# Hybrid attention layer: the multiplication of the softmax weights by 1/row sum moved to ScalarE in both attentions

## What is computed

```python
proj = h @ w_in
# forgetting attention (FoX), 8 heads of 128, causal, blocks of 128 queries
s = einsum('bqhd,bkhd->bhqk', qi, k) * scale + ci - cum_k
p = softmax(where(mask, s, NEG_INF));  o_fox = einsum('bhqk,bkhd->bqhd', p, v)
# sliding window (SWA), 16 query heads of 64, 4 key heads, window 128, a sink per head
s = einsum('bnqhgd,bnkhd->bnhgqk', qb, kk) * d**-0.5 - slope * dist
p = softmax(concat([s, sink]))[..., :-1];  o_swa = einsum('bnhgqk,bnkhd->bnqhgd', p, vv)
y = (o_fox * silu(g_fox)) @ w_br_fox ... ; out = layer_norm(ALPHA * x + gate * (merged @ w_out)) * g + b
```

## Time and profile before

| what | value |
|---|---|
| median of 3 runs | 2979.22 us (2978.62 to 2983.83) |
| profiled execution, its own time | 2981.71 us |
| its span in the trace | 2980.0 us |
| TensorE busy | 2716.4 us, 91% |
| VectorE busy | 1806.2 us, 61% |
| ScalarE busy | 1120.8 us, 38% |
| GpSimd busy | 363.3 us, 12% |
| sliding window attention | about 915 to 1520 us of the span |
| forgetting attention | about 1520 to 2190 us |

### The profile page before, as it was taken

The page is one execution under the profiler, slowest core; times in us unless marked ns, Lnnn a source line. Parts: engine busy times, 40 slices in busy tenths (PEclk is TensorE's granted clock), DMA queues, the critical chain, the costliest instruction groups (busy, mean ns, idle before and its releaser), DMA issues. The chain is left out here.

```text
span 2980.0 us, 39132 instructions
## 1 busy us (share of the span) xinstructions
PE 2716.4 (91%) x12241; PEld 2183.8 (73%) x12241; DVE 1806.2 (61%) x2769; ACT 1120.8 (38%) x2081; POOL 363.3 (12%) x357
## 2 busy tenths in 40 slices
PE   4888999899998999999969999999969999999895
PEld 2367786777876777777758888888747888888684
DVE  5655565895566777777746666566555455644335
ACT  4422234423234444444434444444433332334111
POOL 0200001100010000000001111111130001023002
PEclk9999999999999999999989999999979999999997
DMA  6455542465664333333374443443464454555442
GB/s 227 155 211 218 190 169 99 120 147 149 169 140 103 111 111 111 111 110 111 104 276 106 112 101 93 104 106 90 106 180 134 147 168 168 172 168 177 135 143 102
DMA packets 303094, 421.29 MB, mean 141 GB/s; under 512 B 16256, under 2 KB 227264, under 8 KB 298432
## 3 DMA queue, kind: packets, MB, share of 16 engines
q1 hardware_dynamic: 273504, 353.51, 36.4%
q0 software_dynamic: 16480, 58.75, 10.5%
q10 hardware_dynamic: 13056, 8.39, 1.0%
HBM read 301.05 MB, written 119.55 MB: 141 GB/s over the span
## 5 line engine op out<-in xcount | busy, mean ns | idle before, releaser
L1542 PE MATMUL pA<-b_hi,w_hi 128*128 128x512 f32 x1008 | 401.6, 398 | 64.2 <-DVE ctile L1112 37.0
L1542 PE MATMUL pC<-b_hi,w_hi 128*128 128x512 f32 x1008 | 403.4, 400 | 31.0 <-DVE ctile L1112 16.6
L1542 PE MATMUL pA<-b_hi,w_lo 128*128 128x512 f32 x1008 | 398.9, 396 | 0.0
L1542 PE MATMUL pA<-b_lo,w_hi 128*128 128x512 f32 x1008 | 397.2, 394 | 0.0
L1542 PE MATMUL pC<-b_hi,w_lo 128*128 128x512 f32 x1008 | 396.2, 393 | 0.0
L1542 PE MATMUL pC<-b_lo,w_hi 128*128 128x512 f32 x1008 | 395.4, 392 | 0.0
L1105 DVE TENSOR_TENSOR w_lo<-w_sum,w_hi 128x512 fp32r<-128x512 f32 x336 | 254.5, 762 | 175.9 <-ACT w_hi L758 173.9
L151 ACT CAST w_hi<-w_raw 128x1024 fp32r<-128x1024 f32 x128 | 134.9, 1054 | 424.7 <-PE zP L2209 208.8
L758 ACT CAST w_hi<-w_sum 128x512 fp32r<-128x512 f32 x336 | 208.9, 622 | 202.6 <-DVE w_sum L1100 106.9
L1542 PEld LDWEIGHTS pA<-b_hi,w_hi 128*128 128x128 f32 x1008 | 191.7, 190 | 120.5 <-issue 51.9
L156 DVE TENSOR_TENSOR w_lo<-w_raw,w_hi 128x1024 fp32r<-128x1024 f32 x128 | 159.5, 1246 | 195.4 <-ACT w_hi L151 194.4
(11 more groups left out here) (252 smaller groups left out, 4892.5 us busy)
## 6 DMA issues: line engine op xcount, KB each, us to landing
w_raw<-in_w_in_dram SPq DMA_DIRECT2D x84, 1024.0 KB, 7.6
proj_scratch<-ctile SPq DMA_DIRECT2D x84, 512.0 KB, 2.7
proj_scratch<-ctile POOLq DMA_DIRECT2D x84, 512.0 KB, 5.6
bg_raw<-in_w_ada_dram SPq DMA_DIRECT2D x64, 512.0 KB, 5.1
w_raw<-in_w_out_dram SPq DMA_DIRECT2D x64, 512.0 KB, 3.9
w_raw<-in_w_br_swa_dram SPq DMA_DIRECT2D x32, 512.0 KB, 3.9
w_raw<-in_w_br_fox_dram SPq DMA_DIRECT2D x32, 512.0 KB, 3.8
aux<-proj_scratch SPq DMA_DIRECT2D x64, 256.0 KB, 3.9
```

Source lines behind the costliest of these rows:

```text
L1542: last = nc.tensor.matmul(BANKS[k][:], w[:, j, :], b[:, j, :], start=(k < 4 and n == 0), stop=(n == 11), skip_group_check=True)
```

## The change

The multiplications by `row_inv` leave GpSimd (L703, L715) and VectorE (L1337). ScalarE does them as copies with a scale that is read per partition from `row_inv`: four instructions of 128x256 in each half of a unit, one of 128 x 128(i+1) in each block of a head. In a unit they stand one `after` step behind the exponentials. In a head they stand directly behind the exponential. In the second half of a unit VectorE now forms `row_inv` before its `half_out(0)`, and ScalarE's copies stand before its own `half_out(0)`. GpSimd keeps its DMAs.

```diff
--- before.py
+++ after.py
@@ -696,13 +696,6 @@
                 gate_out(1)
                 group_out(35, 2 * (35 - QKV - 6))
 
-                with pool.Fori(0, 32) as s:
-                    pool.wait_ge(s_inv, s + 1)
-                    for i in range(2):
-                        w = sp_w[:, i].rearrange("p k t -> p (k t)")
-                        last = nc.gpsimd.tensor_tensor(w, w, row_inv[:, i:i + 1].broadcast_to([P, 2 * P]), ALU.mult)
-                    last.then_inc(s_norm, 1)
-
                 for row in range(2):
                     pool.wait_ge(stored[row], 16 * GROUPS)
 
@@ -710,10 +703,6 @@
                     q = 3 * h + Q_FOX
                     dst = 6 * h + B_G
                     for i in range(8):
-                        pool.wait_ge(f_inv, 8 * h + (i + 1))
-                        w = fp_w[:, 0:i + 1].rearrange("p j t -> p (j t)")
-                        nc.gpsimd.tensor_tensor(w, w, row_inv[:, 0:1].broadcast_to([P, (i + 1) * P]),
-                                                ALU.mult).then_inc(f_norm, 1)
                         if i == 2:
                             add_group(q, 0, dst)
                         if i == 3:
@@ -907,6 +896,12 @@
                                                  accum_out=row_sum[:, i:i + 1])
                         nc.scalar.activation(sink_exp[:], sink_exp[:], ACT.Exp).then_inc(s_exp, 1)
 
+                    def normalise(e):
+                        act.wait_ge(s_inv, 2 * u + (e + 1))
+                        for i in range(4):
+                            ins = nc.scalar.activation(sp_w[:, i], sp_w[:, i], ACT.Copy, scale=row_inv[:, i:i + 1])
+                        ins.then_inc(s_norm, 1)
+
                     def turned_high(e):
                         for k in range(2):
                             act.wait_ge(s_turned, 4 * u + (2 * e + k + 1))
@@ -921,11 +916,14 @@
                     at = SWA_AFTER[par]
                     passed(at[0], at[1])
                     exponentials(0)
-                    passed(at[1], at[2])
+                    passed(at[1], at[1] + 1)
+                    normalise(0)
+                    passed(at[1] + 1, at[2])
                     turned_high(0)
                     passed(at[2], at[3])
                     exponentials(1)
                     passed(at[3], at[4])
+                    normalise(1)
                     half_out(0)
                     passed(at[4], at[5])
                     turned_high(1)
@@ -970,6 +968,11 @@
                         nc.scalar.activation(fp_w[:, 0:i + 1, :].rearrange("p j t -> p (j t)"),
                                              sP[:, :, :].rearrange("p a t -> p (a t)")[:, 0:(i + 1) * P], ACT.Exp,
                                              bias=neg_max[:, 0:1], accum_out=row_sum[:, 0:1]).then_inc(f_exp, 1)
+
+                    def normalise(i):
+                        w = fp_w[:, 0:i + 1, :].rearrange("p j t -> p (j t)")
+                        act.wait_ge(f_inv, 8 * h + (i + 1))
+                        nc.scalar.activation(w, w, ACT.Copy, scale=row_inv[:, 0:1]).then_inc(f_norm, 1)
 
                     def turned_high(i):
                         for k in range(i // 4 + 1):
@@ -1001,6 +1004,7 @@
                         if i < 7:
                             q_high(i + 1)
                         exponentials(i)
+                        normalise(i)
                         for n in FOX_AFTER[i]:
                             after(q + n // 7, n % 7, not (last and n >= 14))
                         if i % 2 == 0 and i:
@@ -1331,12 +1335,6 @@
                         dve.wait_ge(s_exp, s + 1)
                         own(nc.vector.tensor_tensor(row_inv[:], row_sum[:], sink_exp[:], ALU.add))
                         nc.vector.reciprocal(row_inv[:], row_inv[:]).then_inc(s_inv, 1)
-                        dve.wait_ge(s_inv, s + 1)
-                        for i in range(2, 4):
-                            w = sp_w[:, i].rearrange("p k t -> p (k t)")
-                            ins = nc.vector.tensor_tensor(w, w, row_inv[:, i:i + 1].broadcast_to([P, 2 * P]),
-                                                           ALU.mult)
-                        ins.then_inc(s_norm, 1)
 
                     def turned_low(e):
                         for k in range(2):
@@ -1357,8 +1355,8 @@
                     turned_low(0)
                     biased(1)
                     passed(at[2], at[4])
+                    normalise(1)
                     half_out(0)
-                    normalise(1)
                     passed(at[4], at[5])
                     turned_low(1)
                     if not last:
@@ -1621,7 +1619,7 @@
 
                             def turn_weights(e):
 
-                                pe.wait_ge(s_norm, 4 * u + 2 * (e + 1))
+                                pe.wait_ge(s_norm, 2 * u + (e + 1))
                                 if e == 0:
                                     pe.wait_ge(s_v, u + 1)
                                 for k in range(2):
```

## The result

| | kernel before | changed kernel |
|---|---|---|
| median | 2981.52 us (2978.62 to 2988.51, 4 runs) | 3043.38 us (3036.15 to 3048.32, 4 runs) |
| ratio | | 1.0198, 95% interval 1.0182 to 1.0215 |
| profiled execution, its own time | 2981.71 us | 3036.15 us |
| its span | 2980.0 us | 3034.5 us |
| sliding window stage, first scores to the wait for v | 622.6 us | 654.7 us |

The change makes the kernel 2.0% slower. The direction was forecast, and the waits that grow were too; the size was not: 3043 us lies outside the range of 2996 to 3036. Of the 54.5 us of span, 32.1 are in the first stage and 25.9 in the second; the rest of the kernel gave back 3.5.

What follows compares the result with a forecast made beforehand. TensorE, nearly always working, was taken as the bound, so what ends its few waits counts. Eight pairs at 2.7 us (+21) and eight heads at 1.97 us (+16) gave +37 us: 3016 us, range 2996 to 3036 for 8 in 10.

Steps and rivals of the forecast that it cites:

- the wait for GpSimd: Forgetting heads: TensorE's wait for GpSimd's multiplication, 4.7 us in all, goes but is no gain.
- (a): Sliding window, first half of a pair's first unit: VectorE's low part starts behind ScalarE's copies, take and rounding, 1.22 us late.
- (b): Sliding window, second half of the first unit: `half_out` and the joins wait behind ScalarE's four copies and oP copy, +1.16 us.
- (c): Sliding window, first half of a pair's second unit: a join comes sooner, the next rounding later; 0.40 us gained.
- (d): Sliding window, second half of the second unit: the `take` of pC comes too late for TensorE's product 5, +0.70 us.
- head, low part of the turned weights: Forgetting heads, blocks 0 and 1: ScalarE's copies delay the low part that TensorE waits for, +0.81 us a head.
- head, `take` of pA: Forgetting heads, block 5: the `take` moves behind ScalarE's wait for the reciprocal and its copy, +1.16 us a head.
- a microsecond there is one of the span: Both attention stages: moving the joins and takes TensorE waits for moves it at once; otherwise it advances 0.23 us a matmul.
- Cheap and dear copies: Rivals on the four copies' cost: 1.20 us, together +22 us, 3001 (chance 0.17); or 2.36 us, +68 us, 3047 (0.13).
- Given back: Rival: later waits in a pair shrink by TensorE's lateness, so only heads cost, about 2995, or no change; chance 0.10.
- VectorE's relief: Rival: multiplications and collisions leave the joins' chain, ScalarE copies in idle time, faster at 2968 us; chance 0.05.
- Counted at nothing: Forgetting heads, blocks 2, 3, 4, 6 and 7: behind the copies stand roundings and takes TensorE doesn't wait for, no cost.

Runs made afterwards that it cites:

- experiment 6: Changed kernel, but in the forgetting heads, blocks 2 and up, ScalarE's copy stands behind its first following take: 3013.08 us, 1.0103 of the kernel before.
- Experiment 7: Kernel before with only sliding window weights on ScalarE, copies one `after` step later than in the change, `half_out(0)` ahead of them: 2960.21 us, ratio 0.9925.
- experiment 3: Changed kernel with ScalarE's order alone put back, oP copied before the four weight copies in a unit's second half: 3008.91 us, 1.0095 of the kernel before.

## Why the prediction was wrong in size

**Bottleneck and waits: right.** The copies' price, the waits that grow and the new wait for pC's `take` came as written. That the wait for GpSimd brings nothing came true, but not for the reason given: it lay on a chain that starts at the DMA of q (experiment 6), and ScalarE inherited it. Set side by side instruction by instruction, TensorE is later by this much in a pair:

| step | forecast | measured |
|---|---|---|
| (a) to product 0 | +1.22 | +1.23 |
| (b) to product 1 | +1.16 | +1.25 |
| (c) first half, second unit | -0.40 | -0.27 |
| (d) product 5 | +0.70 | +1.06 |
| pair | 2.7 | 3.3 |
| head, low part of the turned weights | +0.81 | +0.88 |
| head, `take` of pA | +1.16 | +1.20 |
| head | 1.97 | 2.6 |

The pair's and the head's lines are from periods without a long fall of the clock. (d) is the only step that was clearly mis-sized. Its chain in ScalarE's timeline of the changed kernel:

```profile
1217.08 1.71 ACT L902 ACTIVATE sp_w<-sp_w,row_inv 128x256 f32<-128x256 f32 x4 [1.04 <-DVE row_inv L1337]
1218.82 0.58 ACT L914 COPY so_st<-oP 64x512 f32<-64x512 f32 x1
1219.43 0.59 ACT L763 COPY ctile<-pD 128x512 f32<-128x512 f32 x1
...
1220.95 0.59 ACT L763 COPY ctile<-pC 128x512 f32<-128x512 f32 x1
```

From the first copy to the `take` of pC it is 3.87 us, where I had 1.60 + 0.49 + 0.48 + 1.04 = 3.61. I let four copies and the copy of oP overlap with what follows them as plain neighbours do, 0.40 and 0.49 from start to start; but the oP copy starts only when the copies have ended (1.74 us for the four), and the `take` behind it 0.61 us after it. The same 0.1 us stands in (b). The other 0.1 us comes behind the wait: the next matmul starts 0.31 to 0.34 us after the one that waited, where the others stand 0.23 apart. In the two heads without a fall half a microsecond more lies at two places: 0.16 us at product 5 of the third group, and 0.07 and 0.37 us at the first turn of weights, which waits for the DMA of q. Together, stages less their falls: 32.1 - 6.1 = 26.0 and 25.9 - 7.3 = 18.6 us, 44.6 where the sum had 37 (18.6 us is 2.3 a head; the 2.6 of the table comes from the two heads without a fall).

**The step that failed: "a microsecond there is one of the span".** Outside its waits TensorE was taken to advance by 0.23 us a matmul, whatever the waits do. The rows of before gave a clock of 1.00 and 0.98. The waits that come in every pair and head are 0.2 to 1.6 us long there, and the longest at full clock came once:

```profile
PE tP L1452 <- POOL sp_w L703: 2.1, 1, 2.1
```

I carried that rate over to waits which my own sum had put at 2.5 us, in every pair. Behind such waits the clock fell, nine times in the profiled execution. That is a term of its own, 13.4 us after the one fall of before is taken off, and it was not in the sum, nor in a rival, nor in the range. Without it the median would be about 3030 us by this estimate, inside the range.

**The account for the profiled execution.** Forecast about 3019, measured 3036.15 us. The clean terms bring +7.6, the falls +13.4, and outside the two stages the execution is 3.5 us shorter, which I have no cause for: 2981.7 + 37 = 3018.7, and with these 17.5 us 3036.2. The median is another 7 us higher. The other executions have mean clocks of 0.963 to 0.966 where the profiled one has 0.967, and 0.4% of 3035 us is 12 us, about as much as the slowest is longer. More falls in those runs would explain it, but they have no trace, so this stays argued.

**The rivals.** Cheap and dear copies: refuted by 498 ns. "Given back": refuted, the pairs cost 26 us without the clock. VectorE's relief: wrong for this kernel, but not for the idea. I had it turn at a copy of 0.13 us and put it down as below every row of ScalarE. That was worked out for copies at their given places. Experiment 7 has copies of the same price and gains 21 us. What decided was what stands behind the copies, which the prediction itself had said of step (b) without drawing the consequence: experiment 3 puts 30 of the stage's 32 us on the order of four copies and one copy of oP, and the later places of experiment 7 turn the sign.

**Counted at nothing.** The copies of blocks 2, 3 and 4 are indeed free at the change's places: in head 4 TensorE's lateness stays at 0.95 us from block 1's product with v up to the `take` of pA. Behind block 5 it grows by the 0.16 us above. Experiment 6 moved the copies of blocks 2 to 7 together, so it doesn't say which of them held the load of q up, if one did. The forecast of +0.81 us in blocks 0 and 1 was measured at +0.88 against a common start of the turn.

## What to carry over

When work moves to an engine with free time, look for what stands right behind it in that engine's order, and who waits for that; here 30 us hung on one 0.58 us copy that should have stood ahead of the four new ones, and places one step later, with that copy ahead, turned a loss of 34 us into a gain of 21. When a sum puts a TensorE wait above those that the trace of before shows at full clock, the clock belongs into the range as a term of its own: here each fall cost 1.5 us on top of the wait. The engine that a wait names can be the last link of a chain that starts elsewhere: GpSimd's 4.7 us in the heads hung on a DMA. An idle engine that has a finished tile to take stands in the wrong order: moving one `take` ahead of the exponentials it stood behind gave 24 us in the kernel before and 28 in the one with late copies.

## What the runs showed of the hardware

Behind waits of 1.8 to 3.5 us TensorE's granted clock fell to 0.50: mostly seven or eight matmuls at 0.43 us each instead of 0.23, 1.5 us lost. It did not fall behind every one. Counted over both stages of all thirteen traces, and leaving out the wait for v, none of 255 waits of 1.0 to 1.78 us had a fall behind it, and 54 of 98 waits of 1.79 to 3.7 us had one: 9 of 22 under 1.9 us, 44 of 73 from there to 2.8, and one of three above. In the changed kernel the same wait of 2.6 us had a fall in every other pair (1102.58 yes, 1181.79 no), and with half of the copies two of the eight waits of 1.79 to 1.86 us before product 1 had one. The waits of 1.3 to 1.5 us of the kernel before had none, nor had its two of 1.86 and 2.14 us. Filled with matmuls that nobody reads, the same places had none either, and the kernel became 13.6 us faster by doing more. The forgetting heads of the change, the same code in five kernels, had four to six falls and took 680.4 to 684.1 us, so their number depends on more than the wait; on what, these runs don't tell.
